# Column sums of the modulation vectors: a two-column product per 128 columns, or rows of one PSUM bank turned at the end of the stage

## The reference

```python
mod = c_act @ w_mod[l] + b_mod[l]                     # 1024 -> 6 * 1024
shift_m, scale_m, gate_m, shift_f, scale_f, gate_f = jnp.split(mod, 6, axis=-1)
```

## Time and profile before

| what | value |
|---|---|
| median of 3 runs | 3252.98 us (3251.86 to 3255.18) |
| the profiled execution, own time | 3246.34 us |
| its span, first to last instruction | 3244.5 us |
| busy: PE, PE weight load, DVE, ACT, POOL | 91%, 73%, 52%, 38%, 13% |
| granted PE clock, mean | 0.956 |
| products of L912 | 416, from 127.3 to 2524.1 us |
| DVE products L877 and L880 | 416, mean 486 and 746 ns (median) |

### The profile page before, as it was taken

The page is one execution under the profiler, slowest core; times in us unless marked ns, Lnnn a source line. Parts: engine busy times, 40 slices in busy tenths (PEclk is TensorE's granted clock), DMA queues, the critical chain, the costliest instruction groups (busy, mean ns, idle before and its releaser), DMA issues. The chain is left out here.

```text
span 3244.5 us, 37650 instructions
## 1 busy us (share of the span) xinstructions
PE 2950.4 (91%) x15073; PEld 2353.4 (73%) x15073; DVE 1679.8 (52%) x2334; ACT 1228.2 (38%) x1821; POOL 411.5 (13%) x395
## 2 busy tenths in 40 slices
PE   7898889999979999999798799998999968876995
PEld 4787556888868888887587457886888736554784
DVE  3575665223345555543416554446655354645896
ACT  5324545122243211221535443225322144535884
POOL 4400400000010000002402100000000004202332
PEclk9899999999989999999899899999999988897997
DMA  7861101222114443332610104324656236334962
GB/s 205 147 176 37 24 1 39 63 65 60 55 39 130 120 121 104 117 90 49 95 53 16 24 10 107 98 72 143 186 160 181 72 47 72 150 109 144 374 238 78
DMA packets 397873, 330.15 MB, mean 102 GB/s; under 512 B 38038, under 2 KB 340484, under 8 KB 397572
## 3 DMA queue, kind: packets, MB, share of 16 engines
q1 hardware_dynamic: 384196, 304.56, 33.3%
q0 software_dynamic: 13248, 23.13, 3.5%
q10 hardware_dynamic: 256, 0.07, 0.0%
HBM read 331.96 MB, written 30.33 MB: 112 GB/s over the span
## 5 line engine op out<-in xcount | busy, mean ns | idle before, releaser
L1101 PE MATMUL ps<-ahi,w_hi 128*128 128x512 f32 (+1 forms) x2264 | 770.8, 354 | 6.6 <-DVE w_lo L1128 6.6
L1102 PE MATMUL ps<-ahi,w_lo 128*128 128x512 f32 (+1 forms) x2264 | 768.0, 353 | 0.0
L1128 DVE TENSOR_TENSOR w_lo<-w_raw,w_hi 128x1024 fp32r<-128x1024 f32 (+2 forms) x244 | 352.0, 1444 | 389.9 <-ACT w_hi L1118 388.1
L1101 PEld LDWEIGHTS ps<-ahi,w_hi 128*128 128x128 f32 x2264 | 428.1, 189 | 69.3 <-DVE w_lo L1128 9.8
L1104 PE MATMUL ps<-alo,w_hi 128*128 128x512 f32 (+1 forms) x2264 | 474.1, 352 | 0.0
L1102 PEld LDWEIGHTS ps<-ahi,w_lo 128*128 128x128 f32 x2264 | 428.4, 189 | 59.6
L1118 ACT CAST w_hi<-w_raw 128x1024 fp32r<-128x1024 f32 (+2 forms) x244 | 285.3, 1171 | 488.7 <-PE ps L1104 378.8
L1104 PEld LDWEIGHTS ps<-alo,w_hi 128*128 128x128 f32 x2264 | 376.8, 189 | 58.8
L880 DVE SCALAR_TENSOR_TENSOR vec_acc<-vec_w,csilu,vec_acc 128x512 f32<-128x512 f32 x364 | 257.7, 753 | 10.8 <-DMA vec_w<-in_w_mod 5.7
L1204 POOL TENSOR_TENSOR xsum<-x 128x768 f32<-128x768 f32 (+1 forms) x4 | 7.2, 1801 | 1421.8 <-DVE x L1189 1421.8
L1189 DVE SCALAR_TENSOR_TENSOR x<-ps,mod,x 128x512 f32<-128x512 f32 x80 | 51.4, 668 | 250.6 <-PE ps L1104 235.2
(11 more groups left out here) (525 smaller groups left out, 5299.4 us busy)
## 6 DMA issues: line engine op xcount, KB each, us to landing
vec_w<-in_w_mod SPq DMA_DIRECT2D x128, 512.0 KB, 3.9
w_raw<-in_w_in SPq DMA_DIRECT2D x102, 512.0 KB, 4.3
e_raw<-in_w_gate SPq DMA_DIRECT2D x46, 512.0 KB
e_raw<-in_w_up SPq DMA_DIRECT2D x46, 512.0 KB
e_raw<-in_w_down SPq DMA_DIRECT2D x46, 512.0 KB
w_raw<-in_w_ffn_gate SPq DMA_DIRECT2D x44, 512.0 KB, 3.9
w_raw<-in_w_ffn_up SPq DMA_DIRECT2D x44, 512.0 KB, 3.9
w_raw<-in_w_ffn_down SPq DMA_DIRECT2D x32, 704.0 KB, 4.7
```

What stands on the lines that cost most here:

```text
L1101: pe.matmul(o, whi[:, j, b0 + b, :], hi[:, b, t0:t0 + tn], start=(b == 0), stop=False)
L1102: pe.matmul(o, wlo[:, j, b0 + b, :], hi[:, b, t0:t0 + tn], start=False, stop=False)
L1128: dve.tensor_tensor(wlo[:, j, 0:d.blocks, :], raw_of(d, i, jj), whi[:, j, 0:d.blocks, :].bitcast(F32), ALU.subtract).then_inc(lo_ready[j]. ...
```

## The change

The sums over partitions swap their operands. The *weights* are now a constant: `pick_row` is 47 columns of zeros with ones in column 23, and the slice that starts at column 23 - r, as wide as the stage has rows, is a matrix whose column r is ones. `vec_hi` and `vec_lo` are *moved*, all 512 columns at once, so a product adds the column sums of the chunk as row r of bank 3 and zero to the other rows. A stage of 8 chunks with two vectors has 16 rows, one of 12 chunks 24, and the third 12. All products of a stage accumulate in the one bank: the first starts it, the last stops it. So a block is 4 products for two vectors and 2 for one.

The rows must then be turned, once per stage: one piece after the last block DVE copies them out of PSUM into the first partitions of `vec_acc` (`copied_at`), one piece later PE transposes four tiles of 128 columns back into bank 3 (`turned_at`), and one later DVE adds the bias. `end` is two pieces later than before.

```diff
--- before.py
+++ after.py
@@ -56,6 +56,7 @@
 N_SLOTS = N_BLOCKS * P
 NOWHERE = 1 << 20
 LRU_W = 256
+VEC_ROWS = 24
 BANK = 512
 
 
@@ -180,7 +181,7 @@
 
         ident = sb(root, "ident", [P, P])
         ones = sb(root, "ones", [P, P])
-        ones_r = sb(root, "ones_r", [P, 2], F32R)
+        pick_row = sb(root, "pick_row", [P, 2 * VEC_ROWS - 1], F32R)
         vec1 = sb(root, "vec1", [P, 128])
         vec2 = sb(root, "vec2", [P, 96])
         vec3 = sb(root, "vec3", [P, 78])
@@ -350,7 +351,8 @@
                 def _(dve):
                     ch = Chain(dve, dve_chain)
                     ch.link(dve.memset(ones[:], 1.0))
-                    ch.mark(dve.tensor_copy(ones_r[:], ones[:, 0:2]))
+                    ch.link(dve.tensor_scalar(pick_row[:], ones[:, 0:2 * VEC_ROWS - 1], 0.0, None, ALU.mult))
+                    ch.mark(dve.tensor_copy(pick_row[:, VEC_ROWS - 1:VEC_ROWS], ones[:, 0:1]))
 
                     def mean_of(t):
                         dve.wait_ge(x_in[t].sem, x_in[t].base + 16)
@@ -827,6 +829,8 @@
                 self.acc = sb(c, "vec_acc", [P, self.nv, self.CN])
                 self.hi = sb(c, "vec_hi", [P, self.nv, self.CN], F32R)
                 self.lo = sb(c, "vec_lo", [P, self.nv, self.CN], F32R)
+                self.rows = self.chunks * self.nv
+                self.row = self.acc[0:self.rows, 0, :]
                 self.norm_first = norm_first
                 self.when = [start + n // self.per_chunk * pieces + n % self.per_chunk * pieces // self.per_chunk for n in range(self.steps)]
                 last = [self.when[(k + 1) * self.per_chunk - 1] for k in range(self.chunks)]
@@ -837,7 +841,8 @@
                 self.lo_at = {n + 1: k for k, n in enumerate(last)}
                 self.mm_at = {n + 2: k for k, n in enumerate(last)}
                 assert len(self.hi_at) == self.chunks
-                self.end = last[-1] + 4
+                self.copied_at, self.turned_at = last[-1] + 3, last[-1] + 4
+                self.end = last[-1] + 6
                 self.c0 = {t: t.base for t in (*vec_loaded, vec_used, vec_hi, vec_lo, vec_mm, vec_chain)}
 
             def sem(self, t, n):
@@ -881,14 +886,18 @@
                             m.then_inc(vec_chain.sem, 1)
                     dve.wait_ge(*self.sem(vec_chain, (s_ + 1) * self.STEP * self.nv))
                     dve.sem_inc(vec_used.sem, 1)
+                if n == self.copied_at:
+                    dve.wait_ge(*self.sem(vec_mm, self.chunks))
+                    dve.tensor_copy(self.row, ps[0:self.rows, 3 * BANK:4 * BANK]).then_inc(vec_chain.sem, 1)
                 if n == self.end - 1:
-                    dve.wait_ge(*self.sem(vec_mm, self.chunks))
+                    dve.wait_ge(*self.sem(vec_mm, self.chunks + 1))
                     t0, nt = self.first // P, self.chunks * 4
                     for v in range(self.nv):
-                        src = ps[:, 3 * BANK:3 * BANK + nt * 2 * self.nv].rearrange("p (t v two) -> p t v two", v=self.nv, two=2)[:, :, v, 0]
-                        m = dve.tensor_tensor(self.dst[:, v, t0:t0 + nt], src, self.bias[:, t0:t0 + nt], ALU.add)
+                        src = ps[:, 3 * BANK:3 * BANK + 4 * self.rows].rearrange("p (q k v) -> p k q v", q=4, v=self.nv)[:, :, :, v]
+                        m = dve.tensor_tensor(self.dst[:, v, t0:t0 + nt].rearrange("p (k q) -> p k q", q=4), src,
+                                              self.bias[:, t0:t0 + nt].rearrange("p (k q) -> p k q", q=4), ALU.add)
                     m.then_inc(vec_chain.sem, 1)
-                    dve.wait_ge(*self.sem(vec_chain, self.steps * self.STEP * self.nv + 1))
+                    dve.wait_ge(*self.sem(vec_chain, self.steps * self.STEP * self.nv + 2))
                     for s_ in (1, 2, 4, 5) if self.nv == 2 else (1, 4):
                         if s_ * KT >= t0:
                             dve.tensor_scalar(self.dst[:, 0:self.nv, s_ * KT:(s_ + 1) * KT], self.dst[:, 0:self.nv, s_ * KT:(s_ + 1) * KT], 1.0, None, ALU.add)
@@ -905,11 +914,18 @@
                 if n in self.mm_at:
                     k = self.mm_at[n]
                     pe.wait_ge(*self.sem(vec_lo, k + 1))
+                    for v in range(self.nv):
+                        r = k * self.nv + v
+                        own = pick_row[:, VEC_ROWS - 1 - r:VEC_ROWS - 1 - r + self.rows]
+                        for part in (self.hi, self.lo):
+                            m = pe.matmul(ps[0:self.rows, 3 * BANK:4 * BANK], own, part[:, v, :], start=(r == 0 and part is self.hi),
+                                          stop=(r == self.rows - 1 and part is self.lo), skip_group_check=True)
+                    m.then_inc(vec_mm.sem, 1)
+                if n == self.turned_at:
+                    pe.wait_ge(*self.sem(vec_chain, self.steps * self.STEP * self.nv + 1))
                     for q in range(4):
-                        for v in range(self.nv):
-                            o = 3 * BANK + ((4 * k + q) * self.nv + v) * 2
-                            for part in (self.hi, self.lo):
-                                m = pe.matmul(ps[:, o:o + 2], part[:, v, q * P:(q + 1) * P], ones_r[:], start=(part is self.hi), stop=(part is self.lo))
+                        o = 3 * BANK + q * self.rows
+                        m = pe.transpose(ps[:, o:o + self.rows], self.row[:, q * P:(q + 1) * P], ident[0:self.rows, 0:self.rows])
                     m.then_inc(vec_mm.sem, 1)
 
             def ended(self):
@@ -918,7 +934,8 @@
                 vec_used.base += self.steps
                 for t in (vec_hi, vec_lo, vec_mm):
                     t.base += self.chunks
-                vec_chain.base += self.steps * self.STEP * self.nv + 1
+                vec_mm.base += 1
+                vec_chain.base += self.steps * self.STEP * self.nv + 2
 
         class Dense:
```

## The result

| what | before | after |
|---|---|---|
| median, us (5 runs each, same chip) | 3251.86 (3241.18 to 3255.18) | 3216.81 (3210.90 to 3220.63) |
| ratio, 95% interval | | 0.9893 [0.9874, 0.9912] |
| the profiled execution, own time | 3246.34 | 3210.90 |
| its span | 3244.5 | 3209.1 |
| granted PE clock, mean | 0.956 | 0.956 |

The change takes 35.0 us off where 19.9 was forecast.

The account below looks back on a forecast made before the run. PE was taken to bound all three stages. Savings of 5.2 + 10.4 + 5.2 us less 0.9 for the turn made 19.9 off the median 3252.98: forecast 3233.1 us, range 3227 to 3241.

Parts of the forecast that it names:

- The sums, 16 products into 4: All three stages: a two-vector block falls from 1.79 to 0.92 us, a one-vector block from 0.89 to 0.46.
- The rival of the unhidden loads: All blocks: each product waits for its weight load, pitch 0.33 us, saving only 10.8 us, 3242; chance 0.04.
- The rival of the plain f32 rate: All blocks: 512-column products run in passes at 0.90 us each, 44 us slower, 3297; chance 0.03.
- The turn, 0.9 us for both stages: Stages 2 and 3 (feed-forwards): four transposes on PE cost 0.45 us a stage, without waiting for DVE's copy.
- The first block of stage 1, "counts as 0": Layer 0's input projections: time saved only lengthens PE's wait for a late load, so gain 0 (bound 0.87 us).
- Blocks 3 to 7 of stage 1: Layer 0's input projections, PE busy throughout: each block saves 0.87 us, like those of stage 2.
- I put the tail at 0: Stage 1's eighth block, from PE's first product to DVE's add: 2.84 us against 2.88, so no gain.
- worse case: Stage 1's tail: four products in the slow clock make it 0.8 us worse; fast clock throughout, 0.6 better.
- A block shortened in there … its gain is again about the fast one, 0.87: Stage 1's second block, starting at the lower clock: shortening moves dense work into the slow stretch, gaining about 0.87 us.
- The constant … 0: Start of the kernel: one 128x47 multiply replaces a tiny copy while DVE waits for first loads, costing 0.
- the DMAs are the same: Whole kernel: DMAs, and their order against PE's pieces, are unchanged; no gain or cost was counted.
- PE's wait ahead of the second block near 10 us: Stage 1, sign in the changed trace: PE's wait for DVE's vec_lo, 9.21 us before, would be near 10.

Follow-up runs that it names:

- e15: Changed kernel plus eight two-column products ahead of each block of stage 3 (layer 1's feed-forward): 3215.75 us, 0.9892, on two runs.
- e8: Changed kernel plus one two-column product, into a bank nobody reads, behind each block of stage 3 (layer 1's feed-forward): 3212.88 us, 0.9890.
- e1: New form in stage 1 alone, old form in stages 2 and 3, buffers at 32 modulo 256; against the kernel before: 3248.37 us, 0.9997.
- e9: New form in stage 1 alone, buffers where the kernel before has them modulo 256 (at 96): 1.6 us faster than the kernel before.
- e5: Kernel before with only its constant ones_r made 47 columns wide, so later buffers lie as in the changed kernel: 3238.76 us, 0.9965.
- e6: Changed kernel with 96 unused bytes behind pick_row, so later buffers lie as in the kernel before modulo 256: 3221.89 us, 0.9913.

## Why the forecast was short, point by point

- *The sums, 16 products into 4:* right. 0.92 and 0.47 us for a block, 0.24 behind it; weight loads of 12 to 24 columns (median 98 ns) are hidden. The rival of the unhidden loads is out: all loads use all rows, and the pitch is 0.23 us. The rule of the Trainium skill, "TensorE: Matmul & The Clock Gate", Part 3, on row groups, named in the prediction, does not hold here. The rival of the plain f32 rate, which wanted 0.90, is out as well.
- *The turn, 0.9 us for both stages:* right (0.42 and 0.41 us a stage, no wait); the copy is 0.67 us, hidden.
- *The first block of stage 1, "counts as 0":* right. With the buffers at the old place the second block starts at 154.1 us in the mean of the four kernels with the new form in stage 1, and at 154.5 in the five with the old.
- *Blocks 3 to 7 of stage 1:* right, 17.60 us from block to block for 18.49, 0.87 forecast.
- *"I put the tail at 0":* 0.42 us too good, as the products ran at the lower clock from the first on. The prediction's worse case had 0.8 for this, its better one 0.6 less; both are seen (3.30 here, 2.34 and 2.52 in e15 and e8), and which one comes is luck.
- *"A block shortened in there … its gain is again about the fast one, 0.87":* failed. It took the clock's return for something that comes at a fixed distance. After the long wait it came 6.5 to 8.3 us on with two-column products first, 3.0 to 3.7 with wide ones. That is worth 2.1 us more at the old place (3.0 for 0.87), and with it stage 1 comes to the 7.3 us of the traces.
- *"The constant … 0" and "the DMAs are the same":* failed, and this is the largest step. Their number and order are the same, not their addresses. By the times the place is worth 11.4 us to the old form (clear of the noise) and 6.5 to the new one (not clear); by the traces it is 4.5 to 6.1 at the start of stage 2. The forecast "PE's wait ahead of the second block near 10 us" fell with it.
- *Dense work, priced as unchanged:* it is faster by 4.0 us in stages 2 and 3, by a pitch that has two levels. The few rows of one block that the prediction read, in two decimals, do not show it. That the changed kernel has the shorter pitch in more periods was luck for all that the runs show.

Sum by the traces: 11.8 before stage 2 (form 5.7 to 7.3, place 4.5 to 6.1), 21.3 behind it (14.7 as forecast, 4.0 pitch, 2.6 in sections that vary by several us from trace to trace with no change in them), 33.1 in all for 35.0 timed.

**Left open.** Stage 1's new form alone at the old place measures 1 to 2 us (e1, e9), although its traces are 6.3 and 4.8 us ahead at stage 2. The trace of e1 is of its fastest run, 3238.56 us, 9.8 under its median, so it says little of the others. From stage 2 to stage 3 e9 took 837.9 us, the longest of all traces, e1 831.2, in the middle of them (826.8 to 834.2); whether the first is chance was not tested. With the place moved the same form gives 10.4. What the place is worth behind stage 2 is open as well: timed it is 12.9, the traces have about 5 before stage 2 and 3.4 to 3.8 behind its start, the latter in means of traces that lie up to 10 us apart. Why a transfer is dearer when its target does not start at a multiple of 256, no run shows.

## What to carry to other kernels

A constant that grows by a few bytes moves every buffer behind it, and can move the price of loads with them: before crediting a change with its time, run the old kernel with the new kernel's addresses, and try the big DMA targets at multiples of 256 bytes. The price of a block, added up by instruction, held to the hundredth of a us here, so a remainder this large is a second mechanism, not a mis-sized first one. Read the same dense product's pitch, over a whole period, on both sides before calling the rest unchanged.

## What the runs showed of the hardware

- **DMA targets at 0 modulo 256 bytes of a partition are cheaper.** 275 to 304 ns a packet of q0 in 60 to 160 us at 0 (after, e5), 357 to 368 at 96 (e6, before); PE's longest wait up to the second block is 1.6 to 4.7 us in the nine kernels at 0 and 7.6 to 11.1 in the other nine. Starts at 32, 64 and 96 are all slow.
- **After a wait of 8 to 11 us, the clock returns sooner behind wide products:** 3.0 to 3.7 us after PE resumes with 512-column products (four kernels), 6.5 to 8.3 with 16 two-column ones first (five). After shorter stands of 2.3 to 4.7 us, wide products first (eight kernels), it is 3.4 to 6.1, so the length is not set by the first products alone.
- **Back-to-back 512-column products have two pitches,** 229.0 and 233.3 ns (256 columns: 113.3 and 117.8), fixed from block to block; not chosen by two-column products as such.
